# Depthwise convolution of 31 taps: three channel chunks on VectorE and one on TensorE, in place of two and two

## The reference, cut to what matters

```python
CONV_CH, CONV_K, SWA_HQ = 512, 31, 8

def _conv_module(u, gate, w, b, ln_g, ln_b):        # u, gate: (1, 256, 512)
    a = u * sigmoid(gate)
    y = depthwise causal convolution of a with w (31 taps per channel) + b
    mu = mean(y); var = mean((y - mu)**2)           # over the 512 channels
    yf = (y - mu) * rsqrt(var + EPS) * ln_g + ln_b
    return silu(yf)

def _mixer_even(h, ...):
    z = h @ w_in                                     # u, gate, q, k, v
    a_out = _conv_module(u, gate, ...)
    b_out = _swa_sinks(q, k, v, sinks)               # sliding-window attention, 8 heads
    return concatenate([a_out, b_out]) @ w_out
```

## Time and profile before

| what | us |
| --- | --- |
| median of 3 runs | 1790.89 (1788.59 to 1791.57) |
| the profiled execution, its own time | 1790.24 |
| its span in the trace | 1788.5 |
| TensorE busy | 1708.8 (96% of the span) |
| VectorE busy | 1033.0 (58%) |
| ScalarE busy | 870.3 (49%) |
| GpSimd busy | 82.1 (5%) |
| mean granted TensorE clock | 0.967 of full speed |

### The profile page before, as it was taken

One profiled execution on the slowest core, in us unless ns is written; L12 is line 12 of the kernel. 1 busy time (PEld: TensorE's weight loads), 2 busy tenths in 40 slices (PEclk: granted clock), 3 DMA queues, 4 the chain that ended last, 5 costly groups with the idle time before them and its releaser, 6 DMA issues.

```text
span 1788.5 us, 25741 instructions
## 1 busy us (share of the span) xinstructions
PE 1708.8 (96%) x10539; PEld 1497.2 (84%) x10539; DVE 1033.0 (58%) x1629; ACT 870.3 (49%) x1435; POOL 82.1 (5%) x128
## 2 busy tenths in 40 slices
PE   8897999999989999999999789999999999999998
PEld 7674899988669999799988669999899978769997
DVE  5555566666436666654556745545654554575454
ACT  5564555456445544644355354434544463474343
POOL 3000000000005000000003400000000000000000
PEclk9896999999789999899999899999999999999999
DMA  7341576545115565456654036665556654246652
GB/s 266 118 147 42 177 234 189 186 152 186 50 48 187 179 189 187 154 176 197 186 169 144 27 106 191 187 188 165 190 176 197 182 173 133 84 128 202 188 177 94
DMA packets 200764, 284.03 MB, mean 159 GB/s; under 512 B 9456, under 2 KB 160258, under 8 KB 200648
## 3 DMA queue, kind: packets, MB, share of 16 engines
q1 hardware_dynamic: 199000, 278.42, 49.7%
q0 software_dynamic: 1648, 3.97, 0.7%
HBM read 281.15 MB, written 1.07 MB: 158 GB/s over the span
## 4 chain that ended last, share of the span: by engine, by line
PE 87%; DVE 8%; ACT 4%; issue 1%; DMA 0%; DVEq 0%; ACTq 0%
PE two L1766 78%; DVE w_lo L1196 2%; PE two L1987 2%; PE two L2229 1%; PE two L1838 1%; ACT p_sb L870 1%; PE two L2004 1%; ACT w_hi L713 1%; PE two L1991 1%; DVE act_parts L1213 1%; PE two L2134 1%; DVE p_sb L1396 1%; DVE aux L1642 1%; PE two L1824 1%; DVE aux L1370 1%
## 5 line engine op out<-in xcount | busy, mean ns | idle before, releaser
L1196 DVE TENSOR_TENSOR w_lo<-raw,w_hi 128x1024 fp32r<-128x1024 f32 (+1 forms) x520 | 611.5, 1222 | 221.0 <-ACT w_hi L713 220.2
L1766 PE MATMUL two<-act_parts,w_hi 128*128 128x256 f32 x4096 | 738.7, 283 | 0.0
L1766 PEld LDWEIGHTS two<-act_parts,w_hi 128*128 128x128 f32 x4096 | 637.5, 190 | 6.4 <-issue 2.3
L1766 PE MATMUL two<-act_parts,w_lo 128*128 128x256 f32 x2048 | 578.5, 282 | 0.0
L713 ACT CAST w_hi<-raw 128x1024 fp32r<-128x1024 f32 (+1 forms) x520 | 515.5, 1048 | 14.3 <-DMA raw<-in_ffn_w_up 8.3
L1766 PEld LDWEIGHTS two<-act_parts,w_lo 128*128 128x128 f32 x2048 | 389.6, 190 | 0.0
L1766 PE MATMUL two<-w_hi,act_parts 128*128 128x512 f32 (+2 forms) x1072 | 343.8, 398 | 26.7 <-DVE w_lo L1196 14.8
L1766 PEld LDWEIGHTS two<-w_hi,act_parts 128*128 128x128 f32 x1072 | 204.5, 195 | 77.0 <-DVE w_lo L1196 17.6
L1766 PE MATMUL two<-w_lo,act_parts 128*128 128x512 f32 (+2 forms) x536 | 210.3, 393 | 0.0
L836 ACT ACTIVATE p_sb<-pt_sb 128x512 f32<-128x512 f32 x60 | 37.9, 632 | 313.9 <-DVE pt_sb L1319 252.9
L1766 PE MATMUL two<-w_hi,hid_even 128*128 128x512 f32 x576 | 186.5, 393 | 0.0
(11 more groups left out here) (280 smaller groups left out, 1242.9 us busy)
## 6 DMA issues: line engine op xcount, KB each, us to landing
raw<-in_ffn_w_up SPq DMA_DIRECT2D x160, 512.0 KB, 3.8
raw<-in_ffn_w_down SPq DMA_DIRECT2D x132, 512.0 KB, 3.7
raw<-in_ffn_w_gate SPq DMA_DIRECT2D x80, 512.0 KB, 3.7
raw<-in_a_w_in SPq DMA_DIRECT2D x24, 512.0 KB, 4.6
raw<-in_fox_w_in SPq DMA_DIRECT2D x20, 512.0 KB, 3.8
raw<-in_ffn_w_up SPq DMA_DIRECT2D x32, 256.0 KB, 3.2
raw<-in_ab_w_in SPq DMA_DIRECT2D x14, 512.0 KB, 4.1
raw<-in_w_kv SPq DMA_DIRECT2D x12, 512.0 KB, 3.7
```

The lines of the kernel that those rows point to most:

```text
L1196: nc.vector.tensor_tensor(w_lo[:, r, 0:n], raw[:, r, 0:n], w_hi[:, r, 0:n], ALU.subtract).then_inc(lo_done, 1)
L1766: return nc.tensor.matmul(dst, a, w, start=start, stop=stop, skip_group_check=True)
```

## The change

VectorE computes chunks 0, 1 and 2, with 93 tap instructions in place of 62; TensorE computes chunk 3 alone, and the second set of diagonals, its matmuls and its copy out of PSUM are dropped. The taps on VectorE are handed out as 6, 26 and 25 ahead of the attention (the last as `len(taps) - 36` of 61) and 12 beside each of the pairs 0, 1 and 2. Each tap now waits for one that is three instructions back.

```diff
-DVE_CHUNKS = 2
-PE_CHUNKS = (3, 2)
+DVE_CHUNKS = 3
+PE_CHUNKS = (3,)
@@ gpsimd
             gain_row(norm_g_2[0, 3])
-            diagonals(1, PE_CHUNKS[1])
             alibi(2)
@@ scalar, beside(n)
-                if n == 2:
-                    conv_out(1)
                 if n == 4:
@@ vector, beside(n)
                 if n < 3:
-                    some_taps(6)
+                    some_taps(12)
@@ vector, ahead of the attention
             splits(285)
-            some_taps(20)
+            some_taps(26)
             turned("ABQ", qk[:, 0:4, :], 1, 0, 4).then_inc(t_free[1], 1)
...
             splits(289)
-            some_taps(len(taps) - 18)
+            some_taps(len(taps) - 36)
             attention("swa", beside)
@@ tensor, beside(n)
-                if n < 3:
-                    conv_taps(1, 11 * n, min(11 * n + 11, CONV_K))
                 if n == 3:
-                    pe.wait_ge(cv_pe_out, 2)
+                    pe.wait_ge(cv_pe_out, 1)
```

## The result

The median is 1796.98 us (1785.3 to 1806.67, 20 runs) against 1789.99 (1778.22 to 1793.67, 20 runs). The ratio is 1.0056, with a 95% interval of 1.0036 to 1.0076, so the change is 10.0 us slower (6.4 to 13.6). That is the difference of the means (1797.99 against 1788.02); the medians differ by 7.0. The forecast was 9.9 us and a median of 1800.8. The profiled execution took 1801.38 us, its span is 1799.7.

A forecast was written before the change was run, and what follows sets the result against it. VectorE, not TensorE, was taken to bound the stage: 7.4 us of taps plus 2.5 of lost TensorE clock make 9.9 us, 1800.1 for the profiled execution and 1800.8 for the median, range 1796 to 1806.

The forecast's parts named there:

- The engine that paces the stage: From 993 to 1020 us VectorE paces the attention pairs; TensorE's work there is hidden but for 2.39 us.
- The price of a tap: Each VectorE tap on the path costs 0.397 us, with nothing gained from a distance of three.
- its 12.2 us: VectorE's added time if each tap cost its whole 477 ns; the prediction took 7.4 in its place.
- The covered batch: Second batch, 26 taps for 20: 2.4 us hidden in VectorE's 5.37 us wait, which shrinks to about 3.0.
- A in all: From the first tap behind the last split to the end of `o_lo(0)`: 27.42 us becomes 34.78, plus 7.4.
- The clock up to the mean: TensorE's 4.48 us from `o_lo(0)` to the mean run partly at 1.2 GHz: 2.5 us lost, range 1.7 to 3.1.
- The clock behind the mean: TensorE's turns, values, variance and values after the mean: no loss taken, up to 4.4 us if slow too.
- rival 2: TensorE stays at 1.2 GHz both up to and behind the mean: plus 16.3 us, 1807.2; chance 0.08.
- The start of the output projection: Expected near 1049 us in place of 1039; a start under 1043 would prove the forecast wrong.
- B: Stage part from the end of `o_lo(0)` to the end of the mean: 4.48 us before, plus 2.5 forecast.
- C: Stage part from the end of the mean to the output projection's first matmul; no loss was forecast.

The follow-up runs named there:

- e2: Kernel before without TensorE's chunk 2 (its 31 matmuls and diagonals; those taps left out of the result): ratio 0.9988 to the kernel before, 2.1 us faster.
- e6: Changed kernel with taps ordered chunk by chunk, each waiting for the one right before it: 1800.86 us in its one run.
- e3: Kernel before with the second batch of taps at 32 in place of 20: ratio 0.9981 to the kernel before, 3.4 us faster.
- e4: Changed kernel with the second batch of taps at 32 in place of 26: ratio 1.0033 to the kernel before, 5.9 us slower.
- e1: Changed kernel with TensorE's 31 chunk 2 matmuls put back, result unread: ratio 1.0044 to the kernel before, 7.9 us slower.
- e7: Changed kernel with idle matmuls in TensorE's gaps: ratio 1.0016 to the kernel before, 2.9 us slower.

## Why the prediction was right, and where not

- **The engine that paces the stage.** Right. The chain is VectorE's from 990 to 1025; e2 shows that TensorE's part was hidden but for 2.39 us.
- **The price of a tap.** Right: 12 of them without `alibi` beside them took 4.75 us, 0.396 each. That neither the wait nor the distance of three matters was argued there from the earlier trace rows and is shown now by e6 with the changed kernel: it begins to matter at a distance of one. The Trainium skill, "VectorE: DVE Perf Modes", section "The DRAIN you can't avoid", has the next operation wait until the pipe is empty, but adds that one which is not held starts earlier. The prediction took the first half alone for its 12.2 us. These runs agree with the second half at a distance of two or three (0.397 for operations of 0.477); at a distance of one, where a tap has to wait for the result, starts are 0.52 apart.
- **The covered batch.** Right that it costs nothing, shown twice more (e3, e4). The wait left is 3.43, not 3.0, because GpSimd's diagonals no longer lie beside it: 26 taps took 10.37, 0.396 each, against 0.412 in the earlier trace rows.
- **A in all.** 34.66 us against 34.78 worked out; plus 7.2 against plus 7.4. `alibi` cost 0.49 and 0.50 in its two batches, as before.
- **The clock up to the mean.** The mechanism was right (0.50 from 990.2 to 1030.9), the size 2.8 and not 2.5. It was 1.6, 1.6, 1.7 and 2.3 in e1, e2, e4 and e6, and zero in e3 and in all kernels with fillers (one execution each).
- **The clock behind the mean.** This term of the sum was mis-sized: "with the clock just back, and I take nothing". In the profiled execution it was 3.8 us: the clock came back for 3.2 us and went again while TensorE waited 2.8 us for probs. The earlier trace rows has it holding 1.00 over the same wait, and e1 and e2 lost nothing there, e4 2.5, e3 2.8. It is a term between 0 and 4, and the middle would have been a better value than the lower end; rival 2 had it whole.
- **Why the sum still fits.** 7.2 + 2.8 + 3.8 is 13.9 in these two traces, where 9.9 were forecast for the same stretch. The start of the output projection (1050.15, "near 1049" forecast) hides this, because the changed kernel's execution happened to be 2.8 us ahead at the start of the stage. Over 20 runs of each, the means differ by 10.0 with 3.6 on either side, which holds 9.9 and anything from 6.4 to 13.6. The medians differ by 7.0, and the median of 1796.98 is 3.8 under the forecast of 1800.8 and only 1.0 inside its range (1796 to 1806); 0.9 of the 3.8 is the base, 1790.89 over 3 runs and 1789.99 over 20. That the 9.9 and the 10.0 are so close is luck.

Open: why the same gap of 2.8 us behind the mean costs the clock in one execution and not in another. No run tells it apart, and I didn't try to. Open for the same reason is what the clock costs in the mean of many executions, as against the 6.6 us of these two traces.

## What to carry to other kernels

Find the engine that paces the stage in its own timeline, not in the page's shares: here an engine 96% busy over the kernel was hidden in this stage, and one 58% busy had 61 instructions at 0.397 us with nothing to cover them. Hidden work can still matter through the clock of what stands on the path: nearly half of the loss in the traces (6.6 of 13.9 us) was half clock behind VectorE's longer stretches, and idle matmuls took it back (e7). How much of it the matmuls that were taken away would have saved is not shown: taking them off the old split cost 1.6 us (e2), and putting them back left B at 6.1 (e1). Before moving work between engines, move it in time: 12 taps into a wait that existed, and 22 idle matmuls of 0.46 us each (10.2 us in all) in TensorE's gaps, made the old split 10 us faster.

## What the runs showed of the hardware

- The time of one kernel's runs follows the mean granted clock of TensorE in each: over 25 runs of the kernel before, the correlation is -0.97 and 0.001 of mean clock is worth 1.3 us (clock 0.963 to 0.974, time 1793 to 1778); over the 20 runs of the changed kernel -0.96 and 1.2 us. Nearly all of the 15 to 21 us between runs of a kernel thus goes with the clock. A difference of 2 us between two kernels needs the traces, stage by stage, and one trace of each can mislead: B and C together were 25.3, 22.8 and 21.0 us in three kernels with the same TensorE instructions (the change, e4, e6).
- A VectorE operation of 128x256 that lasts 0.477 us starts 0.397 after the last one when it depends on the second or third before it (before, 6 in 2.38 us; the change, 12 in 4.75), and 0.52 when on the one right before (e6, 25 in 12.98).
- A GpSimd operation of 128x384 beside such taps lengthens them by 0.25 us each (0.50 for two: 12 taps took 5.25 in place of 4.75), and one of 128x128 by about 0.03 (20 taps took 8.31 beside some ten of them and 8.00 without, in e2).
